# A two-layer hybrid encoder trunk on one core: the weight ring is filled by one transfer of 2 MB per buffer in place of two of 1 MB

## The reference, cut to what matters

```python
def swiglu(x, wg, wu, wd):
    return (jax.nn.silu(x @ wg) * (x @ wu)) @ wd

def moe_swiglu(x, router, wg, wu, wd):
    logits = (x @ router).astype(jnp.float32)
    top_val, top_idx = lax.top_k(logits, TOP_K)
    top_w = jax.nn.softmax(top_val, axis=-1)
    ...
    for e in range(N_EXPERTS):
        y = y + gates[..., e:e + 1].astype(x.dtype) * swiglu(x, wg[e], wu[e], wd[e])
    return y
```

## Time and profile before

| | us |
|---|---|
| median of 3 runs | 2239.96 (2235.51 to 2242.16) |
| the profiled execution, device time | 2239.47 |
| its span, first to last instruction | 2237.5 |
| TensorE matmul busy | 2136.9 (96%) |
| VectorE busy | 1454.2 (65%) |
| ScalarE busy | 1234.4 (55%) |
| transfers of the ring (q1) | 478.62 MB, 55.4% of 16 engines' span |

### The profile page before, as it was taken

The page is one execution under the profiler, slowest core; times in us unless marked ns, Lnnn a source line. Parts: engine busy times, 40 slices in busy tenths (PEclk is TensorE's granted clock), DMA queues, the critical chain, the costliest instruction groups (busy, mean ns, idle before and its releaser), DMA issues.

```text
span 2237.5 us, 36196 instructions
## 1 busy us (share of the span) xinstructions
PE 2136.9 (96%) x15346; PEld 1851.9 (83%) x15346; DVE 1454.2 (65%) x1299; ACT 1234.4 (55%) x1155; POOL 22.7 (1%) x24
## 2 busy tenths in 40 slices
PE   8999889999999999988998999999999999999997
PEld 6877778999999787777987888888888888888886
DVE  4633327554443763434745889888888888888884
ACT  4454345344333445435324777777776777677673
POOL 0000100000000000010000000000000000000000
PEclk9999999999999999999998999999999999999999
DMA  5323103334444232211423999989898988989892
GB/s 204 129 65 149 50 3 151 151 151 165 174 165 159 76 113 95 76 40 40 188 114 137 365 351 350 370 329 368 323 377 332 368 344 348 363 331 369 323 377 85
DMA packets 73838, 484.88 MB, mean 217 GB/s; under 512 B 12424, under 2 KB 13576, under 8 KB 15992
## 3 DMA queue, kind: packets, MB, share of 16 engines
q1 hardware_dynamic: 69960, 478.62, 55.4%
q10 hardware_dynamic: 3760, 4.52, 0.6%
HBM read 481.36 MB, written 1.74 MB: 216 GB/s over the span
## 4 chain that ended last, share of the span: by engine, by line
PE 86%; DVE 7%; ACT 3%; DMA 2%; issue 2%; ACTq 1%; SPq 0%; DVEq 0%
PE PS L496 22%; PE PS L498 21%; PE PS L497 21%; PE PS L863 5%; DVE area L1613 3%; PE PS L729 2%; DMA ring<-in_experts 2%; PE PS L747 2%; DVE WL L1613 2%; PE PS L1075 1%; PE PS L1134 1%; PE PS L607 1%; PE PS L1082 1%; PE PS L548 1%; PE PS L771 1%
## 5 line engine op out<-in xcount | busy, mean ns | idle before, releaser
L1613 DVE TENSOR_TENSOR WL<-ring,WH 128x2048 fp32r<-128x2048 f32 x414 | 943.7, 2290 | 305.7 <-ACT WH L1204 167.7
L1539 ACT ACTIVATE WH<-ring 128x2048 fp32r<-128x2048 f32 x336 | 642.9, 1916 | 175.7 <-PE PS L498 143.2
L496 PE MATMUL PS<-WH,XGH 128*128 128x512 f32 x896 | 356.5, 398 | 4.3 <-DVE XGL L1613 3.5
L498 PE MATMUL PS<-WL,XGH 128*128 128x512 f32 x896 | 350.7, 391 | 0.0
L497 PE MATMUL PS<-WH,XGL 128*128 128x512 f32 x896 | 350.3, 391 | 0.0
L1204 ACT ACTIVATE WH<-ring 128x2048 fp32r<-128x2048 f32 x78 | 149.0, 1910 | 140.5 <-PE PS L498 140.4
L498 PE MATMUL PS<-XL,WH 128*128 128x272 f32 (+1 forms) x704 | 202.6, 288 | 0.0
L496 PEld LDWEIGHTS PS<-WH,XGH 128*128 128x128 f32 x896 | 169.0, 189 | 40.2 <-DVE XGL L1613 3.7
L498 PEld LDWEIGHTS PS<-WL,XGH 128*128 128x128 f32 x896 | 168.8, 188 | 36.1
L497 PEld LDWEIGHTS PS<-WH,XGL 128*128 128x128 f32 x896 | 169.1, 189 | 33.9
L496 PE MATMUL PS<-WH,HTH 128*128 128x512 f32 x448 | 176.5, 394 | 0.6
(11 more groups left out here) (306 smaller groups left out, 3568.2 us busy)
## 6 DMA issues: line engine op xcount, KB each, us to landing
ring<-in_experts SPq DMA_DIRECT2D x336, 1024.0 KB, 6.7
ring<-in_weights SPq DMA_DIRECT2D x114, 1024.0 KB, 6.8
ring<-in_weights SPq DMA_DIRECT2D x4, 576.0 KB, 5.9
ring<-in_weights SPq DMA_DIRECT2D x4, 512.0 KB, 4.4
cst<-in_consts ACTq DMA_DIRECT2D x1, 1731.0 KB, 8.7
area<-in_x ACTq DMA_DIRECT2D x2, 512.0 KB, 4.5
out<-area SPq DMA_DIRECT2D x4, 256.0 KB, 2.1
bias_line<-lin SPq DMA_DIRECT2D x1, 672.0 KB
```

What stands on the lines that cost most here:

```text
L496: pe.matmul(o, lh, rh, start=first, stop=False, skip_group_check=True)
L498: return pe.matmul(o, lh, rl, start=False, stop=last, skip_group_check=True)
L1539: act.activation(WH[(BASE + j) % 3][:, :], ring[b][:, 2048 * (j % 2):2048 * (j % 2) + 2048], ACT.Copy).then_inc(S("w_hi"), 1)
L1613: tt = lambda o, a_, b_, op: dve.tensor_tensor(o, a_, b_, op)
```

## The change

A chunk is laid out in memory with 16 KB per partition in one run (the two halves of a partition side by side), and is loaded with one transfer of 128 x 16 KB. Each chunk now adds 16 to its semaphore, and every wait on it counts by 16. Bytes, buffers, order, and the instructions of all other engines stay as they are.

```diff
@@ -362,7 +362,7 @@
         for i in range(len(chunks)):
-            total[i % RING] += 32
+            total[i % RING] += 16
             landed_at.append(total[i % RING])
@@ -402,8 +402,7 @@
                 sp.wait_ge(S("w_lo"), n * HALVES + (2 * i - 2 * RING + 2 + BASE))
-                for half in range(2):
-                    sp.dma_start(ring[b][:, 2048 * half:2048 * half + 2048], experts[e, 2 * i + half, :, :]).then_inc(S(f"landed{b}"), 16)
+                sp.dma_start(ring[b][:, :], experts[e, i, :, :]).then_inc(S(f"landed{b}"), 16)
@@ -466,10 +465,8 @@
-                for half in range(2):
-                    o = CHUNK_AT[(l, name)] + half * P * 4 * width
-                    src = weights[o:o + P * 4 * width].rearrange("(p n) -> p n", p=P)
-                    sp.dma_start(buf[:, half * 4 * width:(half + 1) * 4 * width], src).then_inc(S(f"landed{i % RING}"), 16)
+                o = CHUNK_AT[(l, name)]
+                sp.dma_start(buf[:, 0:8 * width], weights[o:o + P * 8 * width].rearrange("(p n) -> p n", p=P)).then_inc(S(f"landed{i % RING}"), 16)
@@ -1533,7 +1530,7 @@
                 if j % 2 == 0:
-                    act.wait_ge(S(f"landed{b}"), n * (32 * PER_BUF) + (landed_moe0[b] + 32 * (j // 2 // RING + 1)))
+                    act.wait_ge(S(f"landed{b}"), n * (16 * PER_BUF) + (landed_moe0[b] + 16 * (j // 2 // RING + 1)))
@@ -2214,7 +2211,7 @@
-        out[at_:at_ + w.size] = w.reshape(2, tiles, P, -1).transpose(0, 2, 1, 3).reshape(-1)
+        out[at_:at_ + w.size] = w.reshape(2 * tiles, P, -1).transpose(1, 0, 2).reshape(-1)
@@ -2226,7 +2223,7 @@
-    return out.reshape(NE, 2 * len(MOE_ORDER), P, 2048)
+    return np.ascontiguousarray(out.transpose(0, 1, 3, 2, 4)).reshape(NE, len(MOE_ORDER), P, 4096)
```

## The result

The changed kernel takes 2249.51 us as the median of 8 runs (2245.62 to 2252.68), against 2240.03 (2235.51 to 2247.27) before. The ratio is 1.0046, with a 95% interval of 1.0031 to 1.0060: it is slower, by 7 to 13 us. The forecast was 2244.5 us and "about the same", with a range up to 2249.0. The time lies just above the range, and slower is what I gave 0.24.

The account below looks back on a forecast made before the run. TensorE, busy 96% of the span, sets the pace, with ScalarE's queue delaying the start. From the profiled 2239.47 us, +5.2 for the start and -0.7 for the experts gave 2244.0, median 2244.5; 8-in-10 range 2237.5 to 2249.

Parts of the forecast that it names:

- The place and the mechanism: Start, ScalarE's queue: engines alternate packets between queues, so SP's longer runs delay small loads and ScalarE's start, +5.2 us.
- the long issue: Start, ScalarE's queue: issue of the vw2_sb load, 8.88 us before, forecast at 13.8 to 14.3 us.
- The turn: Start: one packet from each queue on an engine; with 16 KB runs forecast at 0.654 to 0.699 us.
- the number of turns: Start: q10's 19.3 turns until the issue ends, taken as unchanged, now 10.2 to 10.7 us in place of 5.25.
- The experts: Expert stage: transfers stay hidden behind TensorE, chunks land slightly earlier or later; taken as -0.7 us.
- the bound of -1.7: Expert stage: largest gain, if the one expert that lost 1.73 us loses less; as much possible on the other side.
- Rival A: All transfers: fewer, larger ones are better and nothing else happens; 2238.3 us, at best 2233; chance 0.07.
- The fit that it named: Skill's transfer cost: 2.0 us fixed plus bytes at 436 GB/s; a pair 8.8 us, one 2 MB transfer 6.8.
- Rival B: Start: it gets no longer, as the stall ends otherwise or runs are cut into 8 KB packets; 2239.3 us; chance 0.13.
- C: Experts' ring: transfer-bound if a 16 KB run exceeds 0.746 us; up to 2677 us; chance 0.05 for any size over 2 us.
- its upper bound: Start: about +10 us of stall, if q10 gets room only when all three first chunks are through.

Follow-up runs that it names:

- f1: Changed kernel with only the first chunk loaded as two transfers (4608-byte runs), second and third whole; 2420.68 us in one run, not comparable, long issue about 11.6 us.
- f2: Changed kernel with the first chunk whole, only the second and third in two transfers (8 KB runs); 4284.93 us in one run, not comparable, long issue about 11.6 us.
- e3: Kernel before with only the memory layout changed to 16 KB per partition, every chunk still loaded as two transfers; 2243.94 us, ratio 1.0015.
- e11: Against e6, each experts' chunk in four 512 KB blocks, loaded by four transfers with 4 KB runs; 2231.02 us, ratio 0.9960.
- e9: Kernel before with whole 2 MB transfers for the 168 experts' chunks alone, layers' chunks still two transfers; 2245.13 us, ratio 1.0026.
- f4: Changed kernel with only the vw1 load of 1024 short runs moved to SP, behind the first three chunks; 2235.44 us in one run.
- e7: Changed kernel with ScalarE issuing vw1 last, behind vw2 and the router's load, which also has 1024 runs; 2248.35 us in one run.
- e6: Kernel before, two transfers per chunk, with the vw1, vw2 and router loads moved to SP behind the first three chunks; 2229.97 us, ratio 0.9963.
- e8: Changed kernel with SP issuing its first three chunks only after ScalarE's nine small loads have landed; 2239.57 us in one run.
- e1: Changed kernel with only the first three chunks back to two transfers each, the other 226 whole; 2246.62 us, ratio 1.0022.

## Why the prediction was wrong, point by point

**The place and the mechanism were right.** The chain starts with the long issue, the counts of packets are equal, and all work behind the stall moved with it. The turn was forecast at 0.654 to 0.699 us and measured at 0.659. That what follows the stall has almost no slack held: 8.7 us more of stall made 8.23 us at the first projection and 7.62 at the second expert. The Trainium skill's page "DMA: Bandwidth & Descriptors", section "Queues, rings and completion order", has the round robin between queue rows, and 170 against 170 packets agree.

**The failed step is the number of turns.** The forecast was 19.3 turns, 10.2 to 10.7 us, for +4.9 to +5.4. What ran was 373 / 16 = 23.3 turns of q1 and 14.05 us (24.85 - 10.8), for +8.7 in the issue. The 19.3 had been counted on q10; on q10 it is now 414 / 16 = 25.9, and on q1 it had been 319 / 16 = 19.9, so the count grew by either queue. Four more turns at 0.66 make 2.6 us of the missing 3.5 (8.7 - 5.2). Eight turns with 9216-byte runs took 2.5 x 16 / 83 = 0.48 us each (81 and 85 packets from 12 to 14.5 us) in place of 0.42, another 0.5. I had taken an average over 16 engines (309 packets in all) as if it were a fixed count that the queue waits for. The other run lengths show that it is not fixed. With quarters q1 had put through only 143 packets, 8.9 turns, from 10.6 us to the end of the issue at 12.2:

```profile
q1 hardware_dynamic: 143, 0.31, 53.1%
```

The pair of issues takes 3.95 us without SP's runs, 4.40 with eighths, 5.51 with quarters, 9.36 to 10.81 with halves, 12.1 mixed and 17.75 to 18.07 whole. This grows faster than in proportion. I suspect that the slowest of the 16 engines decides and that they fall out of step, but no view shows the engines singly, and f1 and f2, made to test it, came out under what this would give. What sets the number of turns stays open.

**The experts were wrong in sign.** I had -0.7, with as much on the other side as the bound of -1.7; it is +2.05 over ten and five executions. I argued from the length of a run. That was right in that the transfers stay under TensorE's pace, and an undisturbed expert takes 125.29 us as before. It was too low in size. From 1250 to 2150 us the changed kernel shows

```profile
q1 hardware_dynamic: 21705, 316.06, 92.8%
```

so a run of 16 KB took 900 x 16 x 0.928 / 19291 = 0.693 us on average, where I had 0.594 to 0.657. (19291 is 316.06 MB in runs of 16 KB.) And I missed that two issues are not the same as one. With pairs there are 18 to 20 waits of ScalarE in four of five executions (40 in e3), with one transfer 37 to 46. But by e3 and e11 more waits do not always mean a longer stretch, so these waits go with the loss and are not shown to be its cause. What in the engines makes the difference no run here tells.

**The sum.** 8.2 and 2.05 make 10.3 us, within the measured 7 to 13. Rival A (larger is better) is refuted by the result and by e9, where whole transfers in the experts are the only difference and the time is longer. The fit that it named is in the section "Anatomy of one DMA — SWDGE (gpsimd) path" of the Trainium skill's page "DMA: Bandwidth & Descriptors", not in "Bandwidth", and is measured on transfers issued by GpSimd; those here are issued by SP. By that fit, as an estimate, one transfer in place of two saves 2.0 us; the trace does not agree, since ScalarE waited 54.1 us for chunks in place of 25.6. Rival B fell with the long issue, and C's 0.746 us for a run was not reached: it was 0.693.

**The range.** The text named +10 us for the stall as its upper bound, and the range left it out. The stall grew by 8.7. With this bound, and nothing gained in the experts, the sum is 2239.96 + 10 = 2250, just above the 2249.51 measured.

## What to carry to other kernels

Look at what shares the DMA engines with a small, urgent load. Here, while two queues had work, they took turns by packet, so the run length of the bulk transfers set the pace of the small ones, and an engine whose next issue stood behind 1024 short runs could not even begin its work. On an engine that has to compute, put at most one such load, and put it last (f4); two of them stall in either order (e7). Or issue them from an engine on which nothing hangs: here that gave 0.4% (e6, 0.9963), about four times the 2.05 us that one or two transfers make in the experts. And where a stage with three buffers runs close to its transfers' pace, two transfers in flight for a buffer did better than one.

## What the runs showed of the hardware that I had not expected

A few microseconds can be won or lost by when the granted clock falls. In e8 the first projection starts 7.8 us sooner than before (24.70 against 32.51), and this lead is lost between 190 and 240 us, where the granted clock is 0.86, that is partly at the lower level of 1.2 GHz:

```profile
190.00:240.00 50.00, 45.99 (x214) 31.08 (x214) 19.49 (x64) 11.79 (x30) 0.00 (x0) 0.86 0.12 43
```

The kernel before does the same work at 1.00:

```profile
198.00:248.00 50.00, 44.91 (x292) 31.84 (x290) 19.67 (x66) 13.54 (x35) 0.00 (x0) 1.00 0.18 68
```

TensorE is busy 44.91 us there, about as in e8, and yet gets through 292 matmuls where e8 has 214. In e6, whose first projection starts at 23.74 us, nothing of this is lost (granted clock 1.00 from 190 to 240). It is not the early start that does it: e3 starts its first projection at 32.21 us, as before, and has 0.85 from 198 to 248. So executions of these kernels differ by several microseconds from the clock alone, which is why differences of 2 us were read from stretches and not from medians, and why the medians of e1, e3 and e9 need not be explained by their transfers alone.
